# Expert weights loaded one expert matrix at a time, in 16 KB rows, instead of a quarter of four experts' matrices in 4 KB rows

## What is computed

```python
g_idx = argmax(h @ w_group + b_group)                      # one of 4 groups
top_v, top_i = top_k(expert logits of that group, 2)       # 2 of its 8 experts
for every expert e:                                        # 32 in a layer
    y_e = (silu(x_e @ w_gate[e]) * (x_e @ w_up[e])) @ w_down[e]
out = sum over the token's two experts of weight * y_e
```

## Time and profile before

| | us |
|---|---|
| median of 3 runs | 1350.68 (1348.88 to 1352.31) |
| the profiled execution | 1349.39 |
| its span, first to last instruction | 1347.4 |
| TensorE busy (matmul) in the span | 928.8 (69%) |
| VectorE, ScalarE, GpSimd busy | 334.6, 176.0, 35.1 |
| data moved | 489.82 MB, mean 364 GB/s |
| mean granted TensorE clock | 0.875 of full |

### The profile page before, as it was taken

The page is one execution under the profiler, slowest core; times in us unless marked ns, Lnnn a source line. Parts: engine busy times, 40 slices in busy tenths (PEclk is TensorE's granted clock), DMA queues, the critical chain, the costliest instruction groups (busy, mean ns, idle before and its releaser), DMA issues.

```text
span 1347.4 us, 15052 instructions
## 1 busy us (share of the span) xinstructions
PE 928.8 (69%) x6198; PEld 400.0 (30%) x6198; DVE 334.6 (25%) x889; ACT 176.0 (13%) x415; POOL 35.1 (3%) x75
## 2 busy tenths in 40 slices
PE   3997888655656647566579999786565656656555
PEld 2774444111111212121248655431111212111212
DVE  2278444202101111112131144531101111102111
ACT  1013331000000000000113245410000000000000
POOL 1000120000000000000000000200000000000000
PEclk8998899888788888788789999998888888788788
DMA  9978439999999999999999357589999999999996
GB/s 345 388 268 326 188 134 362 408 409 410 409 410 409 410 409 410 409 410 409 410 408 405 130 201 299 230 350 409 409 410 409 410 409 410 409 410 409 410 409 269
DMA packets 131739, 489.82 MB, mean 364 GB/s; under 512 B 11489, under 2 KB 11634, under 8 KB 131698
## 3 DMA queue, kind: packets, MB, share of 16 engines
q1 hardware_dynamic: 125632, 486.62, 90.9%
q10 hardware_dynamic: 6066, 2.64, 0.7%
HBM read 488.20 MB, written 1.05 MB: 363 GB/s over the span
## 4 chain that ended last, share of the span: by engine, by line
SPq 61%; PE 20%; DVE 7%; DMA 4%; ACTq 2%; ACT 2%; issue 2%; POOL 0%; DVEq 0%
SPq L406 59%; PE psum L1278 20%; DVE phase_region L927 4%; DMA weight_ring<-in_w_ada 3%; ACTq L552 2%; DMA weight_ring<-in_moe_w_down 2%; SPq L435 1%; SPq L399 1%; ACT h_or_mix_T L587 1%; ACT phase_region L717 0%; ACT phase_region L576 0%; DVE phase_region L859 0%; PE psum L1325 0%; SPq L398 0%; DVE x_tokens L881 0%
## 5 line engine op out<-in xcount | busy, mean ns | idle before, releaser
L1278 PE MATMUL psum<-weight_ring,phase_region 128*32 128x512 f32 (+1 forms) x3456 | 482.6, 696 | 355.2 <-DMA weight_ring<-in_moe_w_gate 136.2
L1278 PEld LDWEIGHTS psum<-weight_ring,phase_region 128*32 128x32 f32 x3456 | 107.2, 122 | 696.6 <-issue 211.9
L1278 PE MATMUL psum<-phase_region 128*128 128x128 bf16 (+4 forms) x1168 | 144.3, 286 | 3.7 <-POOL phase_region L505 0.9
L1278 PE MATMUL psum<-h_or_mix_T,weight_ring 128*128 128x256 f32 (+1 forms) x520 | 116.9, 384 | 8.0 <-ACT h_or_mix_T L587 4.5
L1278 PEld LDWEIGHTS psum<-phase_region 128*128 128x128 bf16 (+3 forms) x1168 | 87.4, 120 | 95.9 <-issue 65.0
L1278 PEld LDWEIGHTS psum<-h_or_mix_T,weight_ring 128*128 128x128 f32 x520 | 99.8, 195 | 23.2 <-DVE h_or_mix_T L868 5.0
L1278 PE MATMUL psum<-weight_ring,h_or_mix_T 128*128 128x512 f32 x224 | 101.4, 604 | 3.4 <-DVE scale L844 3.4
L1144 DVE TENSOR_TENSOR phase_region<-psum,gate_rows 128x512 f32<-128x512 f32 x32 | 22.1, 692 | 234.3 <-PE psum L1278 234.3
L1137 DVE SCALAR_TENSOR_TENSOR phase_region<-phase_region,psum 128x512 f32<-128x512 f32 x16 | 16.9, 1059 | 235.0 <-PE psum L1278 235.0
L1132 DVE SCALAR_TENSOR_TENSOR phase_region<-phase_region,psum 128x512 f32<-128x512 f32 x16 | 11.0, 688 | 256.7 <-ACT phase_region L726 256.7
L726 ACT ACTIVATE phase_region<-psum 128x512 f32<-128x512 f32 x16 | 9.6, 597 | 497.8 <-PE psum L1278 497.8
(11 more groups left out here) (175 smaller groups left out, 464.0 us busy)
## 6 DMA issues: line engine op xcount, KB each, us to landing
weight_ring<-in_moe_w_gate SPq DMA_DIRECT2D x64, 2048.0 KB, 23.8
weight_ring<-in_moe_w_up SPq DMA_DIRECT2D x64, 2048.0 KB, 23.9
weight_ring<-in_moe_w_down SPq DMA_DIRECT2D x64, 2048.0 KB, 23.8
weight_ring<-in_w_ada SPq DMA_DIRECT2D x12, 3072.0 KB, 16.2
weight_ring<-in_w_ada SPq DMA_DIRECT2D x12, 1024.0 KB, 18.3
weight_ring<-in_odd_w_in SPq DMA_DIRECT2D x6, 2048.0 KB, 24.0
weight_ring<-in_even_w_in SPq DMA_DIRECT2D x4, 2048.0 KB, 24.8
weight_ring<-in_even_w_out SPq DMA_DIRECT2D x2, 2048.0 KB, 11.0
```

The source lines that it names most:

```text
L1278: return pe.matmul(out_, lhsT, rhs, start=first, stop=last, **kw)
```

## The change

One DMA still brings 2 MB, and into the same place of the ring, but it is now the whole matrix of one expert: 16 KB in one piece for each of the 128 partitions. The slabs of a matrix kind hold experts 0 and 1, and 2 and 3. TensorE waits for all four matrices before it multiplies any (`all_in`), and signals only at the end of the product (`gate_done`, `up_done`, `down_done`), and SP waits for that before it loads both slabs anew (`slab_free`). Two of the 24 products of a stage stay in quarters with 4 KB rows: the gate of the first quad (`widen_first`, whose first three quarters are signalled one by one) and the down of the last quad (`narrow_last`). For these the loop of four turns becomes two quads written out, a loop of two turns, and two quads written out. Nothing else is touched: the order of the slabs, the size of the DMAs, and the work of ScalarE, VectorE and GpSimd are as before. The first two slabs of the second mixer wait for the end of the last up product where they waited for its second and fourth quarter.

```diff
+        def quarter(n, half):
+            return place(n)[:, half * WIDE * QUARTER:(half + 1) * WIDE * QUARTER].rearrange("p (e n) -> p e n", e=WIDE)
+
+        def slab_free(matrix, quads):
             if matrix < 2:
                 return (gate_done, up_done)[matrix], quads
             return down_done, quads * 2
...
+            LAST = 6 * EP - 2
+
             def load_unit(L, k, half, quad):
 
                 n = MOE0[L] + k
                 src = (gate_src, up_src, down_src)[k % 6 // 2]
-                unit = 2 * (k % 2) + half
-                sp.dma_start(quad_unit(n, half), src[L, :, bass.ds(quad * WIDE, WIDE), unit * UNIT:(unit + 1) * UNIT]).then_inc(
+                sp.dma_start(pair_slab(n)[:, half:half + 1, :],
+                             src[L, :, bass.ds(quad * WIDE + (k % 2 * 2 + half), 1), :]).then_inc(
+                    (slab_in, rest_in)[half][n % RING], 16)
+
+            def load_quarter(L, k, half):
+
+                n = MOE0[L] + k
+                at = (2 * (k % 2) + half) * QUARTER
+                src, quad = (gate_src, 0) if k < 2 else (down_src, EP - 1)
+                sp.dma_start(quarter(n, half), src[L, :, quad * WIDE:(quad + 1) * WIDE, at:at + QUARTER]).then_inc(
                     (slab_in, rest_in)[half][n % RING], 16)
 
             def load_experts(L):
@@ -411,19 +420,35 @@
                 for k in range(RING):
                     sp.wait_ge(*before[len(before) - RING + k][2:])
                     for half in range(2):
-                        load_unit(L, k, half, k // 6)
+                        if k < 2:
+                            load_quarter(L, k, half)
+                        else:
+                            load_unit(L, k, half, 0)
+                for k in range(2):
+                    for half in range(2):
+                        if k + half < 2:
+                            sp.wait_ge(first_quarters, 3 * L + 2 * k + half + 1)
+                        else:
+                            sp.wait_ge(gate_done, EP * L + 1)
+                        load_unit(L, k + RING, half, 0)
 
                 def follow(turn, k):
 
+                    sp.wait_ge(*slab_free(k % 6 // 2, turn * UNROLL + (EP * L + k // 6 + 1)))
                     for half in range(2):
-                        sp.wait_ge(*unit_free(k % 6 // 2, 2 * (k % 2) + half, turn * UNROLL + (EP * L + k // 6 + 1)))
                         load_unit(L, k + RING, half, turn * UNROLL + (k + RING) // 6)
 
-                with sp.Fori(0, EP // UNROLL - 1) as i:
+                for k in range(2, 6 * UNROLL):
+                    follow(0, k)
+                with sp.Fori(0, EP // UNROLL - 2) as i:
                     for k in range(6 * UNROLL):
-                        follow(i, k)
-                for k in range(6 * UNROLL - RING):
+                        follow(i + 1, k)
+                for k in range(6 * UNROLL - RING - 2):
                     follow(EP // UNROLL - 1, k)
+                for k in range(LAST - RING, LAST + 2 - RING):
+                    sp.wait_ge(*slab_free(k % 6 // 2, EP * (L + 1)))
+                    for half in range(2):
+                        load_quarter(L, k + RING, half)
...
-                    sp.wait_ge(*unit_free(k % 6 // 2, 2 * (k % 2) + 1, EP))
+                    if k == LAST:
+                        sp.wait_ge(last_quarters, 2)
+                    else:
+                        sp.wait_ge(*slab_free(k % 6 // 2, EP))
...
-                def widen(matrix, units, xt, done):
-
-                    for unit, (ready, land, w) in enumerate(units):
-                        pe.wait_ge(ready, land)
-                        for k in (2 * unit, 2 * unit + 1):
+                def all_in(slabs):
+
+                    for n, land in slabs:
+                        pe.wait_ge(slab_in[n % RING], land)
+                        pe.wait_ge(rest_in[n % RING], land)
+                    pairs = [pair_slab(n) for n, _ in slabs]
+                    return [pairs[e // 2][:, e % 2, :] for e in range(WIDE)]
+
+                def widen(matrix, slabs, xt, done):
+
+                    w = all_in(slabs)
+                    for k in range(KD):
+                        for e in range(WIDE):
+                            ins = mm(PS[e * SLOT:(e + 1) * SLOT, matrix, :], xt[:, k, e * SLOT:(e + 1) * SLOT],
+                                     w[e][:, k * F:(k + 1) * F], k == 0, k == KD - 1, skip_group_check=True)
+                    ins.then_inc(done, 1)
+
+                def narrow(slabs):
+
+                    w = all_in(slabs)
+                    for h in range(2):
+                        for k in range(KF):
                             for e in range(WIDE):
-                                ins = mm(PS[e * SLOT:(e + 1) * SLOT, matrix, :], xt[:, k, e * SLOT:(e + 1) * SLOT],
-                                         w[:, e, (k % 2) * F:(k % 2 + 1) * F], k == 0, k == KD - 1, skip_group_check=True)
-                        ins.then_inc(done if unit == 3 else part_used[matrix], 1)
-
-                def narrow(units):
-
-                    for k, (ready, land, w) in enumerate(units):
-                        pe.wait_ge(ready, land)
+                                ins = mm(PS[e * SLOT:(e + 1) * SLOT, 6 + h, :], HIDT[:, k, e * SLOT:(e + 1) * SLOT],
+                                         w[e][:, k * D + h * HALF:k * D + (h + 1) * HALF], k == 0, k == KF - 1,
+                                         skip_group_check=True)
+                        ins.then_inc(down_done, 1)
+
+                def quarters(slabs):
+
+                    return [((slab_in, rest_in)[half][n % RING], land, quarter(n, half)) for n, land in slabs for half in range(2)]
+
+                def widen_first(slabs, xt):
+
+                    for part, (arrived, land, w) in enumerate(quarters(slabs)):
+                        pe.wait_ge(arrived, land)
+                        for k in (2 * part, 2 * part + 1):
+                            for e in range(WIDE):
+                                ins = mm(PS[e * SLOT:(e + 1) * SLOT, 0, :], xt[:, k, e * SLOT:(e + 1) * SLOT],
+                                         w[:, e, k % 2 * F:(k % 2 + 1) * F], k == 0, k == KD - 1, skip_group_check=True)
+                        ins.then_inc(first_quarters if part < 3 else gate_done, 1)
+
+                def narrow_last(slabs):
+
+                    for k, (arrived, land, w) in enumerate(quarters(slabs)):
+                        pe.wait_ge(arrived, land)
                         for h in range(2):
                             for e in range(WIDE):
                                 ins = mm(PS[e * SLOT:(e + 1) * SLOT, 6 + h, :], HIDT[:, k, e * SLOT:(e + 1) * SLOT],
@@ -1555,7 +1615,7 @@
                             if k == KF - 1:
                                 ins.then_inc(down_done, 1)
                         if k < KF - 1:
-                            ins.then_inc(part_used[2], 1)
+                            ins.then_inc(last_quarters, 1)
```

More of the change, by code:

```diff
@@ L59, in build_trunk @@
     ROUNDS = -(-(S - SLOT) // SLOT2)
-    UNIT = KD * F // 4
     LAM0 = 0.8 - 0.6 * math.exp(-0.3)
@@ L67, in build_trunk @@
     UNROLL = 2
+    QUARTER = KD * F // 4
     ctx = ExitStack()
@@ L271, in build_trunk @@
         xt_act = sem("xt_act")
-        part_used = [sem(f"{w}_part_used") for w in ("gate", "up", "down")]
+        first_quarters = sem("first_quarters")
+        last_quarters = sem("last_quarters")
         gate_done = sem("gate_done")
@@ new lines, in quad, with slabs @@
+                def quad(i, j, first=False, last=False):
+                    n = i * UNROLL + (EP * L + j)
+                    adds = i * (4 * UNROLL) + (ADDS * L + 1 + 4 * j)
+                    def slabs(matrix):
+                        both = [MOE0[L] + 6 * j + 2 * matrix + half for half in range(2)]
+                        return [(s, i * (16 * GROUP) + landed(s)) for s in both]
+                    pe.wait_ge(xt_dve, i * (4 * UNROLL) + 4 * ((EP + 1) * L + j + 1))
+                    pe.wait_ge(xt_act, i * (4 * UNROLL) + 4 * ((EP + 1) * L + j + 1))
+                    if first:
+                        widen_first(slabs(0), XT[:, j % 2])
+                    else:
+                        widen(0, slabs(0), XT[:, j % 2], gate_done)
+                    y = i * (2 * UNROLL) + 2 * ((EP + 1) * L + j + 1)
+                    pe.wait_ge(y_ready, y - 1)
+                    pe.wait_ge(x_added, adds)
+                    pe.wait_ge(ada_ready, 6 * (L + 1))
+                    combine((j + 1) % 2, adds, y)
+                    widen(1, slabs(1), XT[:, j % 2], up_done)
+                    pe.wait_ge(slots_built, i * (2 * UNROLL) + 2 * ((EP + 1) * L + j + 2))
+                    gather((j + 1) % 2, gathered)
+                    pe.wait_ge(weights_built, n * 2 + 2)
+                    pe.wait_ge(x_added, adds + 4)
+                    turn_weights().then_inc(weights_turned, 1)
+                    pe.wait_ge(hidden_ready, n + 1)
```

(14 more changed lines are left out.)

31 lines of the change are left out of this document (removed).

## The result

The changed kernel takes **1316.7 us** (median of 4 runs, 1314.29 to 1316.81) against 1350.2 for the kernel before (median of 4): a ratio of 0.9746, 95% interval 0.9729 to 0.9763. It is 2.5% faster. 1309 was predicted, 1298 to 1337 as the range.

What follows compares the result with a forecast made beforehand. The prediction took the MoE stages as bound by loads, the mixers by the engines. 1349.4 - 40.3 (cheaper loads) - 1.5 (last product) = 1307.6 us; the profiled execution being 1.3 below the median, 1309, range 1298 to 1337.

Steps and rivals of the forecast that it cites:

- The bound, and that it is the loads: In the two MoE stages, loads bound the kernel: time is the number of DMAs times 5.12 us.
- The price of a 16 KB row: Expert loads: 10 ns fixed cost per packet, so 610 ns per 16 KB packet, 4.88 us a DMA, 40.3 us gained.
- SP and code: SP issues the same DMAs; two more written-out quads add a few instruction packets, fetched in TensorE's idle time.
- The start of a stage: First quad: loads waiting for the first up product go out later, covered by four down loads; no cost, 5 us spare.
- The last quad: End of second stage: TensorE is ready 0.9 us before the last down quarter lands, then finishes it 1.5 us faster.
- The cover of the first stage's end: Last quad of the first stage: any delay is covered by the `w_ada` loads, which last to 688.74 us.
- TensorE keeps up: Within stages: waiting for all four matrices costs nothing, since queued loads cover it, just in time even at 1.2 GHz.
- Rows cut into 4 KB: Rival for the loads: the queue makes 4 KB packets of 16 KB rows, time stays 1349 us; chance 0.09.
- Less overhead saved: Rival for the loads: only 3.7 ns saved per packet, gain 14.9 us, time 1334 us; chance 0.17.
- Large packets slow: Rival for the loads: a 16 KB packet takes 1098 ns, adding 616 us, time 1965 us; chance 0.03.
- The last quad's chain: Rival at the second stage's end: rows cut and TensorE at 1.2 GHz, 12.2 us later, 1363 us; chance 0.05.

Runs made afterwards that it cites:

- e5 to e7: Changed kernel with, in order: whole matrices everywhere and one loop, 1333.43 us; middle loop also written out, 1317.44; only first and last quad written out, 1314.32.
- e8: The changed kernel run once more, nothing altered, beside a repeat of the variant with only first and last quad written out: 1315.8 us.
- e4: Changed kernel with the last down of each stage also brought by whole matrices instead of quarters: 1327.67 us.
- e1: Changed kernel with each matrix still brought whole by one DMA, but set down in the ring in four separate pieces of 4 KB: 1353.55 us.
- e2: Changed kernel with each DMA bringing the same half of two experts' matrices, in 8 KB rows: 1326.88 us.

## Why the prediction was right, and where its sizes were off

**The bound, and that it is the loads:** right. Time in the stages was the number of DMAs times their price before and after.

**The price of a 16 KB row.** The step from "10 ns beside its bytes" to 4.88 us a load was right in kind and 6% too large: 9.4 ns, 4.894 us. The gain is 168 x 0.226 = 38.0 instead of 40.3, **2.3 us less**. Of the three rows behind it the tiny packets with 11.4 ns had been the best guide, as taken; the fit through 2 and 4 KB with 14.7 was inflated.

**"SP and code"**, where the added packets are "fetched in its idle time", was the step that failed. I looked for the cost of the longer code on TensorE, where it is idle, and not on the DMA engines, which are the bound and through which the code comes: **3.0 us** in long groups of this profile. The groups of e5 to e7 support it (0.5, 3.9 and 0.4 us with 28, 52 and 35 packets). In whole times less code brought only 1.6 us, with an error of 0.6, so the price of the longer code as a whole is less certain than the lengthened groups.

**The start of a stage.** No cost was right, but the eight loads there did not bring their full gain. Before, the fourth down load landed 24.1 us after the first was issued in the first stage and 24.4 in the second (the products of a first quarter below, less one load of 5.12); now it is 23.6 and 24.3 (the down products at 239.51 above and at 888.45).

```profile
244.68 1.92 PE L1278 MATMUL psum<-weight_ring,phase_region 128*32 128x512 f32 x16 [1.00 <-DMA weight_ring<-in_moe_w_gate]
...
910.39 1.93 PE L1278 MATMUL psum<-weight_ring,phase_region 128*32 128x512 f32 x16 [1.21 <-DMA weight_ring<-in_moe_w_gate]
```

```profile
888.45 8.77 PE L1306 MATMUL psum<-weight_ring,phase_region 128*32 128x512 f32 x64 [4.62 <-DMA weight_ring<-in_moe_w_down]
```

That is 0.6 us instead of 1.8, **1.2 us less**. e8 has 23.7 and 24.2 in the same two places, so it is not one execution's chance; why these eight loads gain so little is open. The prediction had put the first down product at about 237.5; it began at 239.51, 2.0 us more than four loads at their price and the 2 us allowed for latency. It cost nothing: the next product follows 19.57 us later.

**The last quad:** right in both parts. 0.9 us to spare were forecast and 1.2 found; the 1.5 us from the last product at the full clock came.

**The cover of the first stage's end.** That "this place is covered by the `w_ada` loads" was wrong, as e4 shows: a last product that ends 6.9 us later makes the second `w_ada` product begin 7.1 us later (679.52 against 672.40). In the changed kernel itself it costs next to nothing: from the start on the last quarter to the second `w_ada` product it is 19.4 us, and 19.2 before.

**TensorE keeps up:** right, with 3.97 us or more of idle time before each product that waits for whole matrices, although such a product begins at the lower clock and takes 8.4 to 10.0 us where one at the full clock takes 7.07.

The rest is 0.4 us by which this profile reaches the first stage later than that of before (215.92 against 215.48). The sum for the spans: 40.3 + 1.5 - 2.3 - 3.0 - 1.2 - 0.4 = 34.9 us, which is 1347.4 - 1312.5. That it closes to a tenth is partly luck: the 0.3 us lost at the end of the first stage and 0.3 us by which the second mixer is shorter are not in it and cancel. It holds for one profile of each kernel. By the medians the gain is 33.5 us (1350.2 to 1316.7) where 41.7 was forecast (1350.7 to 1309); the profiled execution is the fastest of the changed kernel's four, and no trace shows what the others lose.

**The rivals.** Rows cut into 4 KB: refuted by 2942 packets, and e1 shows what it would have given. Less overhead saved: refuted by the 611.7 ns of a 16 KB packet and by e2; the saving is 9.4 ns for every packet and not 3.7. By the rule of the Trainium skill ("DMA: Bandwidth & Descriptors", section "Why small descriptors are slow (HBM only)"), about 3 cycles beside 128 for 4 KB, a load would have become 1.7% shorter (an estimate); it became 4.4% shorter, and the measurement decides. The ceiling of 435 GB/s that the same page gives ("Where 436 GB/s comes from") fits: 4096 bytes in 150.6 ns on 16 engines are 435 GB/s, what is left when the 9.4 ns are taken away. That is a rate worked out from the three sizes; the fastest slice on the changed kernel's page has 431. Large packets slow: refuted, 611.7 ns and not 1098. The last quad's chain: it did not decide, with 1.17 us of waiting left before the last quarter.

## What to carry to other kernels

When the DMA engines are the bound and a load is made of 4 KB rows, lay out the transfer so that one partition's row is as long as memory allows: here 8 KB rows brought 2.9% of the loads' time and 16 KB rows 4.4%, and it costs only waits that the queue covers. Keep small pieces at the two places where something waits at once, the first load of a stage that frees a buffer and the last one before its end; here they are worth 9 and 11 us in the run's time. And when loads are the bound, count the instruction packets too: code that is written out comes through the same engines, here 1.6 us, with an error of 0.6, for the code of two quads more.

## What the runs showed of the hardware that had not been expected

- The price of a packet is so regular that three sizes fit one line: 160.0, 310.6 and 611.7 ns for 4, 8 and 16 KB.
- How long an issue holds the SP queue went with the number of packets and not with the bytes. Four DMAs of 2 MB that go out together held it for 11.25 to 12.05 us in e1 (512 packets of 4 KB each), for 1.90 to 2.38 in e2 (256 of 8 KB) and for 1.75 to 1.96 in the changed kernel (128 of 16 KB), with the same waits and the same bytes; these are the groups from 288 to 370 us. As the holding went, the chain moved from SPq 61% to DMA 49% with no change in what bounds the kernel.
- Packets of instructions (16 KB, about 1.1 us each) went with groups of 16 KB loads that were 0.1 to 1.2 us longer in 29 cases and no longer in 93; without one no group was.
